# Three attention blocks on one core: exchange ahead of weight slabs, part of a third down tile, scaling ahead of taps

## The reference

```python
h = x
# block 1: differential attention, 8 heads, softmax(q1 k1) - lam * softmax(q2 k2)
h = h + diff_attention(rms_norm(h), ...)
h = h + conv_ffn(rms_norm(h))          # up 1024 -> 2*2816, 3-tap conv, silu gate, down
h = h + (p[0] @ w_proj) * sigmoid(rms_norm(h) @ w_gate)
# block 2: windowed attention, |i-j| <= 128, 16 query and 4 key heads, with sinks
h = h + windowed_gqa(rms_norm(h), ...)
h = h + conv_ffn(rms_norm(h))
h = h + (p[1] @ w_proj) * sigmoid(rms_norm(h) @ w_gate)
x = rms_norm(h)
# block 3: causal attention with forget gates beside a 31-tap depthwise convolution
proj = rms_norm(x) @ w_in              # conv input, q, k, v, forget, two gates
x = x + (sig(gate_a) * conv(a) + sig(gate_b) * attention(q, k, v, f)) @ w_out
x = x + (silu(g) * u) @ w_ffn_out
```

## Time and profile before

| what | us |
|---|---|
| median of three runs | 2135.21 |
| the profiled execution | 2134.71 |
| its span, first to last instruction | 2132.9 |
| PE busy | 2057.4 |
| DVE busy | 1227.8 |
| ACT busy | 942.5 |
| POOL busy | 902.2 |
| mean granted clock of PE | 0.985 |

### The profile page before, as it was taken

The page is one execution under the profiler, slowest core; times in us unless marked ns, Lnnn a source line. Parts: engine busy times, 40 slices in busy tenths (PEclk is TensorE's granted clock), DMA queues, the critical chain, the costliest instruction groups (busy, mean ns, idle before and its releaser), DMA issues.

```text
span 2132.9 us, 28726 instructions
## 1 busy us (share of the span) xinstructions
PE 2057.4 (96%) x9976; PEld 1694.0 (79%) x9976; DVE 1227.8 (58%) x1842; ACT 942.5 (44%) x1494; POOL 902.2 (42%) x660
## 2 busy tenths in 40 slices
PE   6999999999999989899999999999989999999999
PEld 5778778888887867788888887877778788888887
DVE  7487757546264868856736266538769473213122
ACT  5455545434244566634524245534643444323222
POOL 4422135544555521034555455434114455445453
PEclk9999999999999989999999999999989999999999
DMA  4222123223323210022232223222102232222223
GB/s 148 97 75 75 50 70 99 99 99 99 99 99 99 87 62 31 21 69 91 87 119 93 95 98 109 89 79 80 40 21 99 79 99 89 99 99 94 95 97 109
DMA packets 52612, 183.21 MB, mean 86 GB/s; under 512 B 6432, under 2 KB 6688, under 8 KB 52512
## 3 DMA queue, kind: packets, MB, share of 16 engines
q1 hardware_dynamic: 51072, 177.76, 25.3%
q10 hardware_dynamic: 1440, 4.07, 0.5%
HBM read 176.04 MB, written 2.10 MB: 84 GB/s over the span
## 4 chain that ended last, share of the span: by engine, by line
PE 79%; DVE 14%; issue 3%; ACT 2%; DMA 1%; SPq 0%; ACTq 0%; DVEq 0%
PE PS L530 78%; DVE acc L1588 2%; DVE AR L2091 1%; DVE ptlo L1759 1%; PE PS L753 1%; ACT Bhi L1089 1%; DVE nmax L1707 1%; DVE Blo L1581 1%; DVE nmax L1710 1%; DMA AR<-AR 1%; DVE AR L1751 1%; DVE X L1624 0%; SPq L496 0%; ACT AR L1181 0%; DVE nmax L1718 0%
## 5 line engine op out<-in xcount | busy, mean ns | idle before, releaser
L522 POOL TENSOR_TENSOR wlo<-raw,whi 128x512 fp32r<-128x512 f32 x656 | 902.0, 1397 | 1219.6 <-ACT whi L1068 1218.0
L530 PE MATMUL PS<-Bhi,whi 128*128 128x512 f32 x2368 | 939.4, 397 | 32.9 <-POOL wlo L522 15.0
L530 PE MATMUL PS<-Blo,whi 128*128 128x512 f32 x2368 | 928.0, 392 | 0.0
L530 PE MATMUL PS<-Bhi,wlo 128*128 128x512 f32 x2368 | 927.4, 392 | 0.0
L1068 ACT ACTIVATE whi<-raw 128x1024 fp32r<-128x1024 f32 x328 | 345.4, 1056 | 532.7 <-PE PS L530 431.4
L530 PEld LDWEIGHTS PS<-Bhi,whi 128*128 128x128 f32 x2368 | 448.2, 189 | 142.8 <-issue 31.5
L530 PEld LDWEIGHTS PS<-Bhi,wlo 128*128 128x128 f32 x2368 | 448.3, 189 | 95.5
L530 PEld LDWEIGHTS PS<-Blo,whi 128*128 128x128 f32 x2368 | 448.6, 189 | 90.1 <-issue 0.5
L1572 DVE TENSOR_TENSOR AR<-PS,R 128x512 f32<-128x512 f32 x170 | 115.2, 689 | 237.0 <-PE PS L530 225.4
L1624 DVE TENSOR_TENSOR X<-X,PS 128x512 f32<-128x512 f32 x88 | 60.4, 687 | 230.7 <-PE PS L530 230.0
L1867 DVE SCALAR_TENSOR_TENSOR AR<-AR,par_sb 128x511 f32<-128x511 f32 x88 | 117.4, 1335 | 8.8 <-ACT AR L1295 8.8
(11 more groups left out here) (230 smaller groups left out, 2040.4 us busy)
## 6 DMA issues: line engine op xcount, KB each, us to landing
raw<-in_weights SPq DMA_DIRECT2D x328, 512.0 KB, 3.2
AR<-AR SPq DMA_DIRECT2D x56, 64.0 KB, 2.0
X<-in_xT ACTq DMA_DIRECT2D x4, 512.0 KB, 7.8
out<-X SPq DMA_DIRECT2D x8, 256.0 KB, 3.7
AR<-in_pT ACTq DMA_DIRECT2D x2, 512.0 KB, 3.2
par_sb<-in_parameters ACTq DMA_DIRECT2D x1, 322.0 KB, 4.5
AR<-in_positions ACTq DMA_DIRECT2D x1, 256.0 KB, 9.0
con_sb<-in_constants ACTq DMA_DIRECT2D x1, 198.5 KB, 8.9
```

Of the source, the lines that this page charges most:

```text
L522: ins = pool.tensor_tensor(wlo[:, j, c], raw[:, j % RAWS, c], f32(whi[:, j, c]), ALU.subtract)
L530: return pe.matmul(out, w, x, start=start, stop=stop)
```

## The change

- **First output projection** (DVE): the add of tile m now comes before the low part and the sum of tile m - 1.
- **Down projections** (PE): lead is 2 in place of 3, and the first two chunks of the third tile (`part=2`) run between the first two tiles' early chunks and their last one. `tile` can run a part of a tile.
- **Second attention** (ACT): both high parts of the tiles kq2a come ahead of `used("v2", 0, 0)`. `swap_halves` only waits for its tile; the slab's high part comes later (`replaced`), at the end of the step in which `q_low` of that tile is due (two steps after the tile's end).
- **Third attention**: PE spreads the inverse roots behind the projection half, not ahead of it. ACT makes the high part of the transposed probabilities ahead of the head tile's. DVE scales the head tile ahead of the taps and runs one tap ahead of `normalise` and the others behind it, then `head_norm`, `prob_low` and `head_low`. Before the steps, three taps in place of four, and `head_scaled(2)` ahead of the values' low parts.
- In the first attention nothing changes but a wait that is already met (`swap_halves` on qk1a), and `embedding` uses `replaced` for the same code.

```diff
@@ -544,12 +544,15 @@
                 pe.wait_ge(tile_free[bank], before + 1)
                 return PS[:, bank, :]
 
-            def tile(stage, i, j, hi, lo, nk, ready=None, halfway=None):
+            def tile(stage, i, j, hi, lo, nk, ready=None, halfway=None, first=0, end=None):
 
                 s, slot, _ = slab_of(stage, i, j)
-                weights(s)
-                out = open_tile(stage, i, j)
-                for k in range(nk):
+                bank, _ = tile_of(stage, i, j)
+                out = PS[:, bank, :]
+                if first == 0:
+                    weights(s)
+                    open_tile(stage, i, j)
+                for k in range(first, end or nk):
                     if ready is not None:
 
                         pe.wait_ge(ready[0], ready[1] + k + 1)
@@ -557,7 +560,8 @@
                                hi[:, k, :], lo[:, k, :], k == 0, k == nk - 1)
                     if halfway and k == nk // 2 - 1:
                         halfway()
-                last.then_inc(slab_done, 1)
+                if end is None:
+                    last.then_inc(slab_done, 1)
 
             def norm_sum(norm):
 
@@ -580,7 +584,7 @@
                 last.then_inc(rspread, 1)
 
             def tiles(stage, n, hi, lo, nk, ready, norm=None, lead=2, late=1,
-                      meanwhile=None):
+                      meanwhile=None, part=0):
 
 
 
@@ -604,11 +608,13 @@
                             last.then_inc(slab_done, 1)
                     if ks[0] == 0 and meanwhile:
                         meanwhile()
+                    if ks[0] == 0 and part:
+                        tile(stage, 0, lead, hi, lo, nk, first=0, end=part)
                 if norm:
                     norm_sum(norm)
                 for j in range(lead, 4):
                     tile(stage, 0, j, hi, lo, nk, halfway=(lambda: spread_norm(norm))
-                         if norm and j == lead else None)
+                         if norm and j == lead else None, first=part if j == lead else 0)
                 if n > 8:
                     with pe.Fori(1, n // 4) as i:
                         for j in range(4):
@@ -846,12 +852,12 @@
                 for g in range(steps):
                     if g + AHEAD[kind] < steps:
                         scores(kind, g + AHEAD[kind])
-                    if kind == 3 and g and finished(kind, g - 2) is not None:
-                        head_spread(finished(kind, g - 2))
                     late = kind == 2 and g % 4 == 0
                     if piece(kind, g) and not late:
                         t, part, parts = piece(kind, g)
                         project_qk(PROJ[kind], norm, t - 2 if kind == 3 else t, part, parts)
+                    if kind == 3 and g and finished(kind, g - 2) is not None:
+                        head_spread(finished(kind, g - 2))
                     if kind == 1:
                         if g in OSUMS:
                             output_sums(OSUMS[g])
@@ -918,7 +924,7 @@
                     tiles(f"up{l}.{p}", 2 * n, hi, lo, KC, ready if p == 0 else None,
                           norm if p == 0 else None, late=1 if l == 1 else 2)
                     tiles(f"down{l}.{p}", KC, chunks(Bhi[ab]), chunks(Blo[ab]), n,
-                          (act_split, l * FC + PART0[p]), lead=3)
+                          (act_split, l * FC + PART0[p]), part=2)
 
             def embedding(l):
 
@@ -1075,6 +1081,11 @@
                 if more:
                     high(s + RING, slot, half + RING // RAWS)
 
+            def replaced(stage, j):
+
+                s, slot, half = slab_of(stage, 0, j)
+                high(s + RING, slot, half + RING // RAWS)
+
             def freed(stage, i, j):
 
                 bank, before = tile_of(stage, i, j)
@@ -1151,8 +1162,7 @@
 
             def swap_halves(stage, t, n):
 
-                if stage not in ("qk1a", "kq2a"):
-                    used(stage, 0, t)
+                used(stage, 0, t, False)
                 bank, _ = tile_of(stage, 0, t)
                 if n >= 2:
 
@@ -1240,9 +1250,9 @@
                         exps(kind, g + 1)
                     if kind == 3 and begun is not None:
                         head_square(begun)
+                    prob_high(kind, g)
                     if kind == 3 and halfway is not None:
                         head_high(halfway)
-                    prob_high(kind, g)
                     if kind < 3 and begun is not None:
                         q_high(*place_of(kind, begun))
                     if kind == 2:
@@ -1268,6 +1278,8 @@
                             normed_high(h)
                     if done is not None and kind == 2:
                         swap_halves(PROJ[kind], done, place_of(kind, done)[0])
+                    if kind == 2 and halfway is not None:
+                        replaced("kq2", halfway)
                     if done is not None and kind == 3:
                         used(*qk3(done))
                     if kind == 3 and g == steps - 1:
@@ -1325,8 +1337,7 @@
                         bank, _ = tile_of(f"pp{l}", 0, 4 * q + m)
                         act.activation(pp[:, 4 * q + m, :], PS[:, bank, :], ACT.Copy)\
                            .then_inc(tile_free[bank], 1)
-                    s, slot, half = slab_of(f"pp{l}", 0, q)
-                    high(s + RING, slot, half + RING // RAWS)
+                    replaced(f"pp{l}", q)
                 root(f"ple{l}")
 
                 act.wait_ge(r_ready, NORMS.index(nxt))
@@ -1403,15 +1414,13 @@
 
             root("attn1")
             for t in range(2):
-                used("kq2a", 0, t, False)
                 swap_halves("kq2a", t, QT0[2] + t)
             for t in range(2):
-                s, slot, half = slab_of("kq2a", 0, t)
-                high(s + RING, slot, half + RING // RAWS)
-            used("v2", 0, 0)
+                replaced("kq2a", t)
             for t in range(2):
                 q_high(QT0[2] + t, 0, 1 - t)
-            used("v2", 0, 1)
+            for q in range(2):
+                used("v2", 0, q)
             values("v2", (0,), 0, 256)
             exps(2, 0)
             swap_halves("kq2", 0, QT0[2] + 2)
@@ -1812,18 +1821,14 @@
                         head_inverse(halfway)
                     if g + AHEAD[kind] < steps:
                         maxima(kind, g + AHEAD[kind])
+                    if kind == 3 and begun is not None:
+                        head_scaled(begun)
                     if kind == 3:
-                        taps(TAPS_A_STEP[g % 4])
+                        taps(1)
                     if kind == 2 and begun is not None:
                         rope(PROJ[kind], begun, place_of(kind, begun)[0])
                     if kind < 3 and halfway is not None:
                         q_low(*place_of(kind, halfway))
-                    if kind == 3 and begun is not None:
-                        head_scaled(begun)
-                    if kind == 3 and halfway is not None:
-                        if g:
-                            head_norm(halfway)
-                        head_low(halfway)
                     if kind == 1:
                         for h in OLOW.get(g, ()):
                             normed_low(h)
@@ -1831,7 +1836,13 @@
                         normalise(kind, g + 1)
                     if kind == 1 and begun is not None:
                         rope_add(begun)
+                    if kind == 3:
+                        taps(TAPS_A_STEP[g % 4] - 1)
+                        if g and halfway is not None:
+                            head_norm(halfway)
                     prob_low(kind, g)
+                    if kind == 3 and halfway is not None:
+                        head_low(halfway)
                     if kind == 1 and finished(1, g) is not None:
                         rope_sin(finished(1, g))
                     if kind == 1:
@@ -2013,9 +2024,11 @@
             for h in (6, 7):
                 normed_low(h)
             clear_sum()
-            for m in range(KC):
-                add_half("o1b", m)
-                low_and_add("ffn0", m, m % 2)
+            for m in range(KC + 1):
+                if m < KC:
+                    add_half("o1b", m)
+                if m:
+                    low_and_add("ffn0", m - 1, (m - 1) % 2)
             feed_forward(0)
             embedding(0, "attn1")
 
@@ -2176,9 +2189,9 @@
             ins.then_inc(cc_ready, 1)
             for t in range(2):
                 head_low(t)
-            taps(4)
+            taps(3)
+            head_scaled(2)
             values_low("v3", (0,), T)
-            head_scaled(2)
             head_inverse(2)
             attention(3)
             for c in range(4):
```

## The result

The changed kernel takes **2096.8 us** (median of 4 runs, 2094.9 to 2097.8) where the kernel before takes 2134.1 (4 runs beside them): a ratio of 0.9824, 95% interval 0.9807 to 0.9841. Measured once more it was 2095.5 against 2132.3, ratio 0.983 (0.9813 to 0.9846). I had forecast 2103.0 and a range of 2095 to 2115: the direction and the places were right, the size 6 us too small.

The account below looks back on a forecast made before the run. PE, busy 2057.4 of 2132.9 us, was taken as the bound, so only its idle time and lower-clock losses could be won. Terms summing to 31.7 us took 2134.7 to 2103 us, with an 8-in-10 range of 2095 to 2115.

Parts of the forecast that it names:

- part 3: Start of second attention: high parts ahead of the slab remove the first scores' wait and slow clock; 8.0 us.
- part 1: First attention's output projection: PE's two waits for low parts, 1.40 and 0.94 us, go; 2.3 us.
- part 2: Down projections of the first two blocks: residual adds start earlier, shortening two bank waits before the next stage; 4.0 us.
- part 4: Second attention's later tiles: five PE waits of 1.05 us for the rotation go; 5.0 us.
- the steps after them: Second attention, steps after the last tile: a small gain of 0.5 us.
- part 5: Start of third attention: the 2.61 us wait for the third tile's squares and slow clock go; 5.4 us.
- part 6: Within third attention: four waits for inverse roots and four for squares go; 6.5 us, bounds 2 and 9.
- The other two signs: PE waiting over 0.5 us for the last low part in any down stage; clock at 0.5 for longer than before.
- Rival (c): Start of second attention: first wait stays, low parts held up by GpSimd beyond 748; 2109 us, chance 0.06.
- rival (d): Second attention: put-off slabs hold VectorE up in eight steps, pushing waits past 2.3 us; 2149 us, chance 0.04.
- Rival (a): Both attentions: clock isn't won back, slow stretches follow two or three remaining 2 to 3 us waits; 2109, chance 0.17.
- Rival (b): Second and third attentions: VectorE becomes the bound, only a third of parts 4 and 6 won; 2111 us, chance 0.14.

Follow-up runs that it names:

- after: The changed kernel, with every part of the change made on the kernel before: 2096.8 us, ratio 0.9824.
- c: Only the first output projection's adds changed, on the kernel before: 2129.9 us, ratio 0.9984.
- a: Only the second attention changed (early high parts, exchanges ahead of slabs), on the kernel before: 2117.2 us, ratio 0.9917.
- d: Only the third attention changed (its start and its inner orders), on the kernel before: 2118.3 us, ratio 0.9929.
- e: Changed kernel with both high parts of the second attention's first two query/key tiles behind the values' first slab again: 2099.0 us.
- i: Changed kernel with four taps ahead of the values' low parts and the third tile scaled behind them again: 2103.2 us.
- b: Only the down projections changed, on the kernel before: 2128.1 us, ratio 0.9978.
- after again: The changed kernel, unaltered, measured once more: 2095.5 us, ratio 0.983.
- f: Changed kernel with the slabs of the second attention's later tiles ahead of the exchange again, early high parts kept: 2102.1 us.
- l: Changed kernel plus two slabs replaced two steps later, three chunks in six-chunk down stages, third-attention leftover taps behind the probabilities' low part: 2099.8 us.

## Why the prediction was right, step by step

The terms as forecast and as measured in after's profile (start of the same matmul). New waits are counted with the part that brought them, so the wait of 1.03 at 771.73, with which PE falls back by 1.4 us, is moved here from the table's next column to part 3.

| step | forecast | measured |
|---|---|---|
| first attention, no edit | 0 | -1.3 |
| part 1, adds | 2.3 | 3.0 |
| part 2, down projections | 4.0 | 4.2 |
| part 3, start of the second attention | 8.0 | 8.0 |
| part 4, five later tiles | 5.0 | 5.1 |
| the steps after them | 0.5 | 4.3 |
| part 5, start of the third attention | 5.4 | 5.7 |
| part 6, within it | 6.5 | 10.1 |
| sum | 31.7 | 39.0 |

The forecast was right: the places and the mechanism held, the time lies in the range and near its low end. What was mis-sized are two terms, the steps after the last tile and part 6. One sign that I had named as wrong did appear: a wait on qklo and one on ptlo in the second attention where there was none (1.66 and 1.03 us). My own sum had set 3.4 us aside for them, so they say nothing against it. The other two signs stayed away (PE waits 0.26 us for the last low part, and the loss to the clock went from 32 to 17 us).

**Part 1.** Both waits went, 2.34 us, and 0.6 us more that I had not counted: here a wait costs more than its bracket. In the kernel before the matmul before the wait of 1.40 starts at 303.52 and the one behind it at 305.31, 1.79 us apart where 0.225 is the rule; the one after that comes 0.34 later. That is 1.7 us for a wait of 1.40, so 0.3 us on top, twice here. It isn't so everywhere: in part 4 the waits of 1.05 give back 1.0 us and no more, since PE there now meets the bank just as it comes free and its first matmul still starts late (0.32 us behind the one before, 781.25 to 781.57, where 0.12 is the rule).

**Part 2.** The chain started 1.5 us earlier, as worked out. I had put the new wait at 0.1 to 0.2 us in each of the two stages; it is 0.42. The moment of the low part was right (ends 638.28, PE starts 638.33, a wait of 0.26); the missing 0.16 is the restart again. The gain on the two long waits was 1.9 and 1.8 rather than 1.5 and 1.7. The second of them was followed by slow matmuls, which I took as 1.0 us. Which of the two is, changes from execution to execution: with this code unedited the granted clock over the 5 us behind the first wait was 1.00 (before), 1.00 (c), 0.67 (a) and 0.69 (d), behind the second 0.69, 0.69, 0.66 and 1.00 (d's second wait was only 1.88 us long). So each of the four had at least one slow stretch, a two, and a's stage pair is 1.5 us longer than the one profile I worked from, c's and d's the same. With the edit neither wait was followed by one, and the pair is 4.0 to 4.4 shorter in nine executions.

**Part 3.** All steps stand: the high parts ahead of the DMA (the low parts end at 744.6; forecast 747.6, less the 3.3 us by which all is earlier there), first scores on time, 5.36 us and the slow clock behind it gone (clock 1.00 from 745 to 750, before 0.52), the next wait 2.35 where I had 3.0, and new waits of 0.46, 1.66 and 1.03, 3.15 in all. (The prediction isn't of one piece here: its text says 1 to 3 us, its sum takes off 3.4.) 5.36 + 1.83 - 3.15 = 4.0 is idle time, so 4.0 of the 8.0 are left for the clock, forecast 4.8. Rival (c), that the first wait stays, is out; e shows what it would have cost, 6.1 us, near its 5.5.

**Part 4.** The five waits went for 1.0 us each, as forecast. The slabs two steps later cost nothing in those steps, as their cover (VectorE idle 1.21 us there) promised; rival (d), slower through them, is out. What I mis-sized is what I hardly sized: **the steps after the last tile**, 0.5 forecast and 4.3 measured. In them PE's waits sum to 9.4 us before and 6.9 after. The rest is clock, and it scatters: in kernels whose code is the same there, the whole stage was 4.8 to 9.7 us shorter than before. So of the 4.3 only the 2.5 of idle time is shown by its rows; in a the whole stage still gained 9.7, in i 4.8.

**Part 5.** The wait of 2.61 went, the next became 0.72 (forecast 0.9). (My terms, 2.6 + 3.2 - 0.5, make 5.3, not 5.4.) 5.7 us against the one profile of before; against other executions with the old code there (a, b, c and i, 1.2 to 1.3 us shorter) it is 4.4. The 3.2 us of clock that I added were thus 2 on average.

**Part 6.** The step that failed in size: 6.5 forecast, 10.1 measured, outside my bound of 9. Of idle time 10.6 us became 5.0, a gain of 5.6; forecast 6.5. (Two waits for the inverse, 0.72 and 0.95 us, are left, and the one for the probabilities' low part only shrank, to 2.34.) The term that I had wrong is the clock: I had put it at 2 to 3 us and then left it out of the sum. The stage of before loses 8.9 us to it, that of after 5.1 (all between 1525 and 1536), so 3.8 more; the last 0.7 is in neither. Other executions bear it out: where the orders are old (a, b, c) the stage loses 6.8 to 12.0 us to the clock, where they are new (after again, d, e, f, i) 1.7 to 5.1.

**The clock as a whole.** I had 9.0 us for it and 22.7 for idle time. It gave at most 15 (32 to 17) of the 39; PE's busy time, which leaves idle stretches out, says 13.8, and idle time gave 25.1. Rival (a), the clock is not won back, was the wrong worry: waits of 2 to 3 us do remain, and in after and after again one (2.35 at 762.06) leaves the clock alone and one (2.34 at 1525.83) is followed by 0.5. Rival (d) also took 2.3 us as the length from which the clock falls; the runs show no such limit (last section). Rival (b), VectorE becomes the bound, is false for the change as a whole, but l suggests it for what is left in the third attention.

## What to carry to other kernels

When work is moved in one engine's queue, look at the same pair of operations in every other queue: a low part ahead of the probabilities on one engine and its high part behind them on the other costs more than either order by itself (about 9 us here), and an edit taken back alone can be worse than the kernel before. Price a wait as its length, up to 0.3 us more if PE comes to find the work ready with room to spare, and the half clock that may follow; where many short waits go from one stage, count the clock in the sum and not beside it. A delay through a shared resource moves with the work that causes it, so put that work where the other engine idles, and read the stage after it before counting the gain.

## What the runs showed of the hardware

The length of a wait alone doesn't decide whether the clock falls. Windows of PE (stretch, length, busy, granted clock, DMA share, GB/s) in after, behind the wait of 2.35 us that ends at 762.06, and behind the one of 2.34 that ends at 1525.83:

```profile
762.00:767.00 5.00, 4.60 (x28) 1.00 0.01 3
...
1528.00:1533.00 5.00, 5.00 (x29) 0.50 0.00 0
```

The second execution of the same kernel shows the same two levels (1.00 from 761 to 766, 0.50 from 1528 to 1533), that is 2.4 and 1.2 GHz. In after, PE had waits of 0.22, 0.29 and 0.95 us within 12 us ahead of the second wait, and ahead of the first none for 10 us. But what the program does around a wait doesn't decide it either. In a, the same wait of 2.35 us in the same code, at 767.09, is followed by a slow stretch:

```profile
767.00:772.00 5.00, 4.91 (x21) 0.66 0.01 3
```

The waits of 1.66 and 1.03 us behind it are not to be seen in a, and the stage is as long as in after (9.5 and 9.4 us shorter than before), so there the slow clock only filled time in which PE would have waited. Ahead of the stage pp, with the code unedited, waits of 2.29 and 2.37 us (before and c) had 1.00 over the 5 us behind them, waits of 2.32 and 2.38 us (a and d) 0.67 and 0.69. A wait of 2.18 us (after, 885.55) was followed by 0.66, the same one in after again, 2.16 us, by 1.00. The waits of 2.58 to 2.61 us at the start of the third attention were followed by slow matmuls in all five executions that have them (0.56 to 0.70 over 5 us), and even a wait of 3.77 us (in f, at 760.41) cost only part of a stretch, a granted clock of 0.67 from 761 to 766 and 1.00 behind it. So with waits of 2.2 to 2.4 us one kernel comes out either way from execution to execution, and one profile can't price the clock behind such a wait. What in the execution decides it stays open.
